# The down bias of the experts as two matmuls per expert, and the first expert weights loaded earlier, in a hybrid attention and mixture-of-experts layer

## What is computed

```python
def reference(x, ...):                       # x: (1, 512, 1024) float32
    h = rms_norm(x, g_attn)                  # then attention: group A (indexer, top 128 keys), group B (differential)
    x = x + concatenate([y_a, y_b]) @ w_o
    x = x + moe(rms_norm(x, g_ffn), ...)
...
def moe(h, ...):                             # 32 experts, 4 per row, softmax over the 4 chosen
    ...
    gu = xb @ w_gu[e] + b_gu[e]              # 1024 -> 2048
    glu, lin = minimum(gu[:, :1024], 7), clip(gu[:, 1024:], -7, 7)
    act = glu * sigmoid(1.702 * glu) * (lin + 1.0)
    return (act @ w_down[e] + b_down[e]) * g[:, None]      # summed over each row's 4 experts
```

## Time and profile before

| what | value |
|---|---|
| median of 3 runs | 1443.8 us (1442.34 to 1444.7) |
| profiled execution | 1444.39 us, its span 1442.6 us |
| TensorE busy | 1346.2 us (93%) |
| VectorE (DVE) busy | 1257.3 us (87%) |
| ScalarE (ACT) busy | 1121.1 us (78%) |
| expert weights loaded | 384 chunks of 1024 KB |
| HBM traffic | 322 GB/s over the span |

### The profile page before, as it was taken

How to read it: one execution, slowest core, us unless ns; L and a number is a source line. 1 busy time by engine, 2 the same in 40 slices (tenths; PEclk the granted TensorE clock), 3 DMA queues, 4 the chain that set the end, 5 groups by cost and what they waited for, 6 DMA issues and landing times. The chain is left out here.

```text
span 1442.6 us, 18459 instructions
## 1 busy us (share of the span) xinstructions
PE 1346.2 (93%) x6570; PEld 1086.7 (75%) x6570; DVE 1257.3 (87%) x1314; ACT 1121.1 (78%) x1227; POOL 216.1 (15%) x143
## 2 busy tenths in 40 slices
PE   6999878999999999998999899999899989998995
PEld 5887766776788877876787677777678767876784
DVE  4799778548899999999999899999999999998995
ACT  5666664455787998898888888888888988888874
POOL 1112000012111131111121011210111111210221
PEclk9999979999999999999999999999999999999998
DMA  5422111148999999999999999999999999999991
GB/s 152 146 74 59 45 59 45 44 165 305 332 384 367 378 415 407 382 402 395 393 392 395 398 391 381 396 399 386 396 382 388 390 387 390 388 392 386 399 398 53
DMA packets 85924, 448.50 MB, mean 311 GB/s; under 512 B 18496, under 2 KB 23616, under 8 KB 36608
## 3 DMA queue, kind: packets, MB, share of 16 engines
q1 hardware_dynamic: 73424, 428.32, 74.7%
q0 software_dynamic: 9792, 18.90, 5.4%
q10 hardware_dynamic: 2608, 0.01, 0.1%
HBM read 440.89 MB, written 23.07 MB: 322 GB/s over the span
## 5 line engine op out<-in xcount | busy, mean ns | idle before, releaser
L840 DVE TENSOR_TENSOR whl<-wraw,whl 128x2048 fp32r<-128x2048 f32 x384 | 863.3, 2287 | 69.9 <-ACT whl L835 68.4
L835 ACT ACTIVATE whl<-wraw 128x2048 fp32r<-128x2048 f32 x384 | 727.6, 1916 | 135.1 <-PE ps L2164 87.5
L2164 PE MATMUL ps<-whl,xT 128*128 128x512 f32 x2672 | 640.0, 394 | 11.6 <-DVE whl L840 9.8
L2164 PEld LDWEIGHTS ps<-whl,xT 128*128 128x128 f32 x2672 | 493.8, 188 | 128.2 <-DVE whl L840 17.1
L2164 PE MATMUL ps<-whl,aT 128*128 128x512 f32 x1264 | 304.0, 396 | 7.5 <-DVE whl L840 7.5
L2164 PEld LDWEIGHTS ps<-whl,aT 128*128 128x128 f32 x1264 | 236.4, 190 | 60.5 <-DVE whl L840 12.2
L1030 POOL DMA_INDIRECT out_dram<-ysb,idx x32 | 85.3, 2667 | 646.0 <-ACT ysb L1345 629.9
L1021 POOL DMA_INDIRECT xg<-h_rows,idx x32 | 83.5, 2611 | 230.4 <-DVE idx L1795 227.0
L1907 PE MATMUL ps<-W,HT 128*128 128x512 f32 (+1 forms) x184 | 73.1, 397 | 5.7 <-DVE W L612 4.7
L1909 PE MATMUL ps<-W,HT 128*128 128x512 f32 (+1 forms) x184 | 70.1, 381 | 0.0
L1908 PE MATMUL ps<-W,HT 128*128 128x512 f32 (+1 forms) x184 | 69.8, 379 | 0.0
(11 more groups left out here) (296 smaller groups left out, 1408.1 us busy)
## 6 DMA issues: line engine op xcount, KB each, us to landing
wraw<-in_w_gu_dram SPq DMA_DIRECT2D x256, 1024.0 KB, 15.8
wraw<-in_w_down_dram SPq DMA_DIRECT2D x128, 1024.0 KB, 13.5
WR<-in_w_in_dram SPq DMA_DIRECT2D x20, 512.0 KB, 3.6
WR<-in_w_o_dram SPq DMA_DIRECT2D x8, 512.0 KB, 3.9
xs<-in_x_dram SPq DMA_DIRECT2D x4, 512.0 KB, 7.7
WR<-in_x_dram SPq DMA_DIRECT2D x4, 512.0 KB, 3.5
out_dram<-WR SPq DMA_DIRECT2D x4, 512.0 KB, 2.6
h_rows<-WR SPq DMA_DIRECT2D x4, 512.0 KB, 2.6
```

The source lines that it names most:

```text
L835: act.activation(whl[:, n % HL, 0, :], wraw[n % RAW], ACT.Copy).then_inc(chunk_hi, 1)
L840: eng.tensor_tensor(whl[:, n % HL, 1, :], wraw[n % RAW], whl[:, n % HL, 0, :].bitcast(F32), ALU.subtract).then_inc(chunk_lo, 1)
L2164: ins = pe.matmul(bank, a[x_][j], w[:, b, j, 512 * q:512 * q + 512], start=c == NG and j == 0 and n == 0, stop=last and j == nj - 1 and n ...
```

## The change

The dense bias rows are gone: their matmuls, ACT copies and accumulating DMAs, and all waits that counted them. In their place `down` begins with 2 matmuls per expert, the same table with the down part of the bias rows, and the down chunks add to that. The table has two buffers now (`sel`), since it is read twice, and `pick_gu` stands in another place on ACT. `find_gates` for the first two experts moves from before expert 0's bias to after its chunk 2, and `turn_g` from after chunk 0 to there too; the turned gates go to the other turning bank, and `turn_x(1)` waits for their lower half. On DVE the first three lower halves and `turn_x_lo` stand before `spread_gates`. On SP chunks 0 to 3 are loaded one row tile earlier, once the last tile's second-group scores are done; chunks 4 and 5 stay.

```diff
-DENSE_AT = [(0, 3), (0, NG), (1, 1), (1, 5)]
...
-        sel_gu = place("sel_gu", [P, P], F32R, offset=o_qb + 64032)
+        sel = [place(f"sel{n}", [P, P], F32R, offset=o_qb + (64032 if n else 62976)) for n in range(2)]
...
+                sp.dma_start(xres, x[0, rows_of(t), :]).then_inc(xres_in, 16)
+                if t == T - 2:
+
+                    sp.wait_ge(score_ps, SCORE[("score", NO[(T - 1, 7)])] + 1)
+                    for c in range(4):
+                        load_chunk(sp, 0, 0, c)
                 if t == T - 1:
...
-                sp.dma_start(xres, x[0, rows_of(t), :]).then_inc(xres_in, 16)
-                if t == T - 1:
-
-                    for c in range(6):
+                    for c in range(4, 6):
                         load_chunk(sp, 0, 0, c)
...
-            def add_dense(t):
-
-                pool.wait_ge(yrow_ok, t + 1)
-                after(pool, scattered, 16 * t)
-                pool.dma_start(out[0, rows_of(t), :], ysb, accum_op=ALU.add).then_inc(scattered, 16)
...
             def pick_gu(r, e):
 
-                after(act, bias_mm, E * r + e)
+                after(act, down_bias, E * r + e - 1)
...
-                    if is0(r) and c == 4:
-                        turn_g_hi()
-                    if is0(r) and c == 7:
-                        dense_rows(0)
-                    if c == 5:
-                        slots(r, 2)
                     if c == 6:
                         pick_gu(r, 1)
+                        slots(r, 2)
+                    if is0(r) and c == 7:
+                        turn_g_hi()
...
                     if i + 1 < E:
                         turn_x_hi(r, i + 1)
+                        pick_gu(r, i + 1)
...
                 if is0(r):
                     read_counts()
+                    for c in range(3):
+                        split_lo(dve, 0, 0, c)
+                turn_x_lo(r, 0)
+                if is0(r):
                     spread_gates()
-                    split_lo(dve, 0, 0, 0)
-                turn_x_lo(r, 0)
-                for c in range(1 if is0(r) else 0, NG):
+                for c in range(3 if is0(r) else 0, NG):
...
+                if is0(r) and j == 1:
+                    pe.wait_ge(gT_lo, 1)
...
-            def dense_bias(t):
-
-                pe.wait_ge(gT_lo, 1)
-                after(pe, yrow_ok, t)
-                for q in range(2):
-                    cols = slice(2 * DE + 512 * q, 2 * DE + 512 * q + 512)
-                    for a in range(2):
-                        ins = pe.matmul(ps[:, DN + q, :], gT[0:2 * E, a, rows_of(t)], bgs[0:2 * E, cols],
-                                        start=(a == 0), stop=(a == 1))
-                ins.then_inc(dense_ps, 1)
...
-                    if is0(r) and i == 0 and c == 0:
+                    if i == 0 and c == 2:
+                        for j in range(2):
+                            pe.wait_ge(idx_ok, E * r + j + 1)
+                            find_gates(r, j)
+                    if is0(r) and i == 0 and c == 2:
                         turn_g()
-                    if is0(r) and (i, c) in DENSE_AT:
-                        dense_bias(DENSE_AT.index((i, c)))
...
-                    pe.wait_ge(yrow_ok, T + E * r + e)
+                    after(pe, yrow_ok, E * r + e)
+                for q, bank in enumerate(banks):
+                    first = 2 * DE + 512 * q
+                    ins = pe.matmul(bank, sel[e % 2], bgs[:, first:first + 512], start=True, stop=False)
+                ins.then_inc(down_bias, 1)
```

More of the change, by code:

```diff
@@ L560, in build @@
         gT_lo = sem("gT_lo")
-        dense_ps = sem("dense_ps")
+        down_bias = sem("down_bias")
         xg_clear = sem("xg_clear")
@@ L1024, in scatter @@
             def scatter(r, e):
-                pool.wait_ge(yrow_ok, T + E * r + e + 1)
-                pool.wait_ge(scattered, 16 * (T + E * r + e))
+                pool.wait_ge(yrow_ok, E * r + e + 1)
+                after(pool, scattered, 16 * (E * r + e))
                 if not is0(r):
@@ L1047, in pool_round @@
                 for i in range(E + 2):
[L1048 to L1052, removed]
                     if is0(r) and i == E:
@@ L1265, in pick_gu @@
             def pick_gu(r, e):
-                after(act, bias_mm, E * r + e)
+                after(act, down_bias, E * r + e - 1)
                 if e < FIXED:
-                    act.activation(sel_gu, pick[:, e:e + 1].to_broadcast([P, P]), ACT.Copy).then_inc(pick_ok, 1)
+                    act.activation(sel[e % 2], pick[:, e:e + 1].to_broadcast([P, P]), ACT.Copy).then_inc(pick_ok, 1)
                     return
@@ L1274, in pick_gu @@
                 if narrow(e):
-                    act.activation(sel_gu, left, ACT.Copy, scale=col).then_inc(pick_ok, 1)
+                    act.activation(sel[e % 2], left, ACT.Copy, scale=col).then_inc(pick_ok, 1)
                 else:
-                    act.activation(sel_gu, col.to_broadcast([P, P]), ACT.Copy).then_inc(pick_ok, 1)
+                    act.activation(sel[e % 2], col.to_broadcast([P, P]), ACT.Copy).then_inc(pick_ok, 1)
             def fold_table():
@@ L1294, in y_low_half @@
                 act.wait_ge(chunk_used, done(r, e, NCH - 1))
-                act.wait_ge(scattered, 16 * (T + E * r + e))
+                after(act, scattered, 16 * (E * r + e))
                 act.activation(fold_y.rearrange("p (a n) -> p a n", a=2), ps[:, DN:DN + 2, :],
@@ L1301, in turn_g_hi @@
                 act.wait_ge(gT_ps, 1)
[L1302 to L1309, removed]
+                act.activation(gT[:, 0, :], ps[0:3 * E, TP + 1, :], ACT.Copy).then_inc(gT_hi, 1)
             def turn_x_hi(r, j):
@@ L2164, in chunk_products @@
                             ins = pe.matmul(bank, a[x_][j], w[:, b, j, 512 * q:512 * q + 512],
-                                            start=c == NG and j == 0 and n == 0,
+                                            start=False,
                                             stop=last and j == nj - 1 and n == len(parts) - 1)
@@ L2191, in gate_up_bias @@
                 for q, bank in enumerate(banks):
-                    ins = pe.matmul(bank, sel_gu, bgs[:, 512 * q:512 * q + 512], start=True, stop=False)
-                ins.then_inc(bias_mm, 1)
+                    ins = pe.matmul(bank, sel[i % 2], bgs[:, 512 * q:512 * q + 512], start=True, stop=False)
             def gate_up(r, i):
@@ L2247, in pe_round @@
                 turn_x(r, 0)
-                for j in range(2):
-                    pe.wait_ge(idx_ok, E * r + j + 1)
-                    find_gates(r, j)
                 if is0(r):
```

26 lines of the change are left out of this document (8 added, 18 removed).

## The result

The changed kernel takes **1446.8 us** (median of 18 runs, 1445.3 to 1449.3) where the kernel before, run beside it, takes 1443.3 (18 runs, 1440.5 to 1446.2). The ratio is 1.0023, 95% interval 1.0017 to 1.0030: slower by 3.5 us, a little over what can be told from no change, where 3.0 us less was forecast. The profiled execution took 1448.8 us with a span of 1447.1 (before: 1442.6); it is one of the slower of the 18, 2.0 us above their median.

What follows compares the result with a forecast made beforehand. TensorE bounds 350 to 481 us, the DMA queue from about 485. Terms 0.3 - 0.85 - 2.95 + 0.2 + 0.95 = -2.35 at the load of 481.1, about -3.0 with the queue: 1440.8 us; 8-in-10 range 1437.8 to 1445.6.

Steps and rivals of the forecast that it cites:

- Order on DVE: Lower halves before the gates' spread: same DVE work in another order, 0; load 8 issued about 342.0 instead of 346.5.
- Start of expert 0: TensorE's start: +0.6 for load 8 meeting the gather (bounds 0 and +6.0), -0.3 for the gates' picks, together +0.3.
- Loads 0 to 3: Early chunk loads, one tile earlier: worth nothing, since ACT waits for no load from 347.5 to 480.5 us.
- Within expert 0: TensorE: first dense group gone, -1.47; gates' picks now between chunks 2 and 3, +0.6; together -0.85 us.
- Second dense group: At 372.69, before a bias that waits for the activation in any case: removing it gives 0.
- Third and fourth groups: Dense groups on TensorE costing 1.49 and 1.48: removing them gives -2.95 us.
- first two down biases: New down-bias matmuls of experts 0 and 1, before the load of 481.1: +0.95 us.
- DVE follows: DVE's last down chunk of expert 0 nearly keeps up with the earlier TensorE: +0.2 (bounds 0 and +1.5).
- The queue adds 0.65: At the load of 481.1 the DMA queue, freed of four accumulating transfers, turns -2.35 into about -3.0 us.
- 30 biases covered: The other 30 down biases lie beside the full DMA queue: 0; uncovered they would cost 14 us.
- the first gather falls into load 8: Rival: expert 0's gather lands 6.0 us later, TensorE starts late, total +2.4, 1446.2 us; chance 0.09.
- a first product after 350: Sign in the changed profile that would show the gather rival; forecast first chunk product at 347.7 to 348.5.

Runs made afterwards that it cites:

- e1: The change with VectorE's order of before at the experts' start (gates' spread first, one lower half, then turned rows): 1443.1 us, ratio to before 0.9990.
- e2: The change whole, VectorE order kept, but SyncE holds load 8 until the first gather has landed: 1444.5 us, ratio 1.0000.
- e8: The kernel before with only loads 0 to 3 issued early, in the last but one token tile: 1444.3 us, ratio 1.0003.
- e9: e4 with five filling matmuls on TensorE in the pause ahead of expert 1's bias: 1442.0 us, ratio 0.9983.
- e11: e1 with five filling matmuls on TensorE in the pause ahead of expert 1's bias: 1441.6 us, ratio 0.9983.
- e7: e1 without the down-bias matmuls (its rows lack the down bias): 1439.9 us (6 runs), ratio 0.9973.
- e4: e1 with loads 0 to 3 back in the last token tile, as before: 1442.1 us, ratio 0.9983.
- e5: e1 with each pair of down-bias matmuls issued three times: 1443.5 us, ratio 1.0000.
- e10: e4 with the change's VectorE order but one lower half ahead of the turned rows in place of three: 1449.3 us (5 runs), ratio 1.0040.
- e3: Order of e1, but SyncE holds loads 6 and 7 until expert 0's row numbers are known: 1447.2 us, ratio 1.0018.
- e6: The change whole with 40 in place of 20 filling matmuls ahead of the first turned rows: 1446.7 us, ratio 1.0018.

## Why the prediction was wrong

The forecast was 1440.8 us, the result 1446.8. By its own steps:

- *Order on DVE: 0.* **This step failed, with the next.** It counted VectorE's own time, and that was right: e1 and the change have the same lower halves. It did not ask who works beside the moved instructions. The first lower half now runs when GpSimd starts the gather and holds it: landing +1.65 us, first chunk product +1.33 (e2). And it said of load 8 only that nobody is short of it.
- *Start of expert 0: +0.3 (gather +0.6, picks -0.3).* **Measured +5.74.** The gather's term was a choice near the lower end of 0 to +6.0, on the ground that the gather had a lead of 1.7 us over load 8 (by its own rows 344.68 less 4.3 is 340.4, so 1.6). In fact, held on GpSimd until 343.97, it had no lead: the load was issued at 342.86. Loads beside it cost 1.85. The 2.56 us of the clock had no term at all; TensorE's pause was expected to be short, so nothing was said of what a long one does. The picks gave their 0.3 in the change (2.70 us from the turn to the first chunk product in e2, before 3.02), but not in e1, where the first chunk product waits for VectorE's part of the turned rows instead (0.17 us) and comes at 7.60 as before.
- *Loads 0 to 3: 0.* Right (e8, and e9 against e11).
- *Within expert 0: -0.85.* -1.10 by e1 (its activation at 32.04 us after the gather's start, before at 33.14). With the picks that e1 doesn't gain at the start the forecast was -1.15.
- *Second dense group: 0.* Right for what TensorE must do, as the bias waits for the activation in any case. It overlooked that the pause behind it grows from 0.75 to 1.87 us, and three profiled executions lost 1.6 us there.
- *Third and fourth groups -2.95, first two down biases +0.95, DVE follows +0.2.* Right: from expert 0's activation to the load of 481.1 e1 gains 1.94 us (105.86 against 107.80), where these terms give 1.80. The two biases alone cost 0.47 + 0.43 = 0.90 us (e7 against e1), where 0.95 was forecast. Together, without the gather, the terms make -2.95 at that load; e1 and e4 measure -3.03 and -3.07. (The third and fourth group, 1.49 and 1.48, make 2.97 and not 2.95.)
- *The queue adds 0.65.* Not seen. After that load e1 kept 2.9 us of its 3.0 to the end of its profiled execution, e4 2.1, and the means of e1, e4, e9 and e11 lie 1.8 to 2.6 us under before. The last load is issued 2.4 us earlier in e1 and 1.3 in e4, so the queue takes up a part of the gain rather than adding to it.
- *30 biases covered.* Right (e5).

The rival "the first gather falls into load 8", at 0.09, named the place, the sign to look for (a first product after 350) and nearly the time, 1446.2. That its 6.0 us come so near the 5.74 is luck: the load was a cause for 1.85 of them, the hold on GpSimd and the clock, which it did not have, made the rest. Its row for ("every gather under load in this trace") was the evidence to weigh; its row against (the lead of 1.7 us) was worked out for a GpSimd that nobody disturbs. The trace of before held the contrary: the second gather is 1.02 us on GpSimd beside VectorE's small operations, the third 2.43 beside a lower half. I had read the gathers' time to landing and not their length on the engine.

## What to carry to other kernels

When an instruction is moved on one engine, list what runs on every other engine at its new place, above all a GpSimd transfer that someone is waiting for: let no long two-input VectorE operation be under way when it starts, and keep new loads out of its few microseconds. A late operand can cost TensorE twice, once in the wait and once in the clock behind it (here behind 3.98 us and more, not behind 2.54), so a range for a wait on TensorE should hold both. And matmuls that are removed from a pause may have been its filler: a few cheap ones there cost nothing.

The best versions here are the change with VectorE's order of before, e4, and with the filler, e9 and e11: 2.1 to 2.6 us under the kernel before by the medians (0.17%), and some 5 us under the change. The three cannot be told apart.

## What was not expected of the hardware

**A gather of GpSimd that starts while VectorE's two-input operation runs is held until that ends.** In the change the first lower half ends at 342.82 us and the gather's instruction at 343.97; in e2 340.45 and 341.59; in e10 339.76 and 340.90: each time 1.14 us behind the end of the half, whatever follows on VectorE. Of the 31 later gathers of the change 25 end 0.86 to 0.93 us behind a half's end and are 2.4 to 3.0 us long. Two were held by two halves in a row and took 4.62 us; others with the same spacing of the halves were held by the first alone, and what decides between the two is not shown. A memset of GpSimd beside the second half took its usual 0.96 us.

What counts is which of the two is first. A gather that starts with no half running is not held by one that starts behind it, and that half is not longer either. Three gathers of the kernel before and four of the change are of this kind, 0.99 to 1.05 us long, with a half that starts 0.07 to 0.51 us into them. One of before, with the half beside it:

```profile
1002.48 1.04 POOL L1021 DMA_INDIRECT xg<-h_rows,idx  x1 [11.90 <-DVE idx L1795]
```

```profile
1002.55 2.29 DVE L840 TENSOR_TENSOR whl<-wraw,whl 128x2048 fp32r<-128x2048 f32 x1 [0.80 <-ACT whl L835]
```

In the change the half starts 0.44 us ahead of the gather (340.54 against 340.98). No run here tried it just behind the gather's start.

The Trainium skill, page "SBUF — State Buffer", section "SBUF: two separate sides", has a rule of this kind: GpSimd writes a transfer's descriptors through a port pair that it shares with VectorE, and the one that starts first holds the pair for the full instruction while the other is blocked. It puts a VectorE operation with two SBUF inputs against those of GpSimd's instructions that read SBUF, as the gather does for its row numbers (`idx`); the page "GPSIMD Engine Reference", section "Specifications", names such operations without that condition. The trace agrees for the gather, with 2.99 us against 1.28, but not for VectorE: a half that starts while GpSimd writes a gather takes its 2.29 us all the same, and the second and third halves of the change start on time. That the shared pair is the cause is the page's account; no run here separates it from another. Of the figure in the first page, some 0.1 us from VectorE's end to the end of the blocked transfer, the trace shows 0.92 to 1.14: nearly the whole length of an undisturbed gather (1.04, and 1.28 for the first) still follows.

**TensorE's clock after a pause.** Behind 4.50, 4.35 and 3.98 us of idle time (the change, e10, e3) the turn took 1.93 or 1.94 us, at a granted clock near 0.5, the lower level of 1.2 GHz; behind 2.54 (e2) it took 1.06, at 2.4 GHz. Behind 1.87 us on expert 1's bias the clock held in the profiles of the change, e1, e3, e4, e5 and e10, and fell in those of e2, e6 and e7. So one execution says little about a pause of that length.
